# Moving the norm chains to the head of the next block, and regrouping the readout and one decay map in an RWKV-7 recurrence

## The reference, cut to what matters

```python
def rms_norm(x, g):
    y = xf * lax.rsqrt(jnp.mean(xf * xf, axis=-1, keepdims=True) + RMS_EPS)
...
    h_lat = h_lat + gt_m * o_lat
    f_lat = rms_norm(h_lat, norm_ffn[i]) * (1.0 + sc_f) + sh_f
    h_lat = h_lat + gt_f * swiglu(f_lat, ff_w1[i], ff_w3[i], ff_w2[i])
...
# RWKV-7: features, the chain of states, the readout
kk = kk / jnp.maximum(jnp.linalg.norm(kk, axis=-1, keepdims=True), NORM_EPS)
decay = _heads(jnp.exp(-jnp.exp(w_log)))
a = _heads(jax.nn.sigmoid((a0[:, None, None, :] + lora_a).astype(f32)))
...
S = (S * w_t[:, :, None, :] + sa[..., None] * (kk_t * a_t)[:, :, None, :]
     + v_t[..., None] * k_t[:, :, None, :])
...
yn = ((y - mean) * lax.rsqrt(var + LNX_EPS)).reshape(B, T, D) * lnx_g + lnx_b
bonus = jnp.sum(jnp.sum(r[None] * k_dir * r_k, axis=-1, keepdims=True) * v[None], axis=0)
g = jax.nn.sigmoid((h + xx * mu[5]) @ g1) @ g2
return ((yn + bonus.reshape(B, T, D)) * g).astype(h.dtype) @ wo
```

## Time and profile before

| what | us |
|---|---|
| median of 3 runs | 2176.03 |
| lowest and highest | 2170.07, 2177.54 |
| profiled execution, own time | 2173.98 |
| its span, first to last instruction | 2172.1 |
| PE busy in the span | 1988.3 (92%) |
| DVE, ACT, POOL busy | 1230.3, 836.8, 379.3 |
| recurrence, first to last step | 419 to 862 |

### The profile page before, as it was taken

How to read it: one execution, slowest core, us unless ns; L and a number is a source line. 1 busy time by engine, 2 the same in 40 slices (tenths; PEclk the granted TensorE clock), 3 DMA queues, 4 the chain that set the end, 5 groups by cost and what they waited for, 6 DMA issues and landing times. The chain is left out here.

```text
span 2172.1 us, 52627 instructions
## 1 busy us (share of the span) xinstructions
PE 1988.3 (92%) x22423; PEld 1739.4 (80%) x22423; DVE 1230.3 (57%) x1921; ACT 836.8 (39%) x1407; POOL 379.3 (17%) x394
## 2 busy tenths in 40 slices
PE   5799997789999988979999999997979898999998
PEld 3688886678888887979999999996635476888887
DVE  4765445667767763458756667564775434333333
ACT  2433334565565532344323324233335424422321
POOL 0000000766766652120000000022200010000000
PEclk8799998899999999989999999997989998999999
DMA  9577775101111001411212222212100023333332
GB/s 318 180 239 231 228 237 144 41 19 39 32 39 39 20 12 47 151 59 59 78 59 78 63 74 69 68 39 69 59 20 1 0 68 96 96 105 89 96 107 79
DMA packets 226985, 192.76 MB, mean 89 GB/s; under 512 B 13386, under 2 KB 211668, under 8 KB 226388
## 3 DMA queue, kind: packets, MB, share of 16 engines
q1 hardware_dynamic: 226452, 188.84, 28.1%
q0 software_dynamic: 320, 0.79, 0.2%
HBM read 171.38 MB, written 17.43 MB: 87 GB/s over the span
## 5 line engine op out<-in xcount | busy, mean ns | idle before, releaser
L539 DVE TENSOR_TENSOR ffn_lo<-ffn_raw,ffn_hi 128x1024 fp32r<-128x1024 f32 (+1 forms) x58 | 77.5, 1336 | 196.0 <-ACT ffn_hi L534 196.0
L563 PE MATMUL banks<-operand_hi,ffn_w_hi 128*128 128x384 f32 x464 | 155.7, 336 | 10.9 <-DVE operand_lo L505 10.9
L563 PE MATMUL banks<-operand_lo,ffn_w_hi 128*128 128x384 f32 x464 | 155.6, 335 | 0.0
L563 PE MATMUL banks<-operand_hi,ffn_w_lo 128*128 128x384 f32 x464 | 155.5, 335 | 0.0
L563 PE MATMUL banks<-mix_hi,proj_hi 128*128 128x386 f32 (+1 forms) x384 | 136.9, 356 | 15.4 <-DVE proj_lo L755 10.5
L563 PE MATMUL banks<-operand_hi,ffn_hi 128*128 128x512 f32 x352 | 138.4, 393 | 10.7 <-DVE operand_lo L505 8.4
L534 ACT CAST ffn_hi<-ffn_raw 128x1024 fp32r<-128x1024 f32 (+1 forms) x60 | 68.3, 1139 | 189.6 <-PE banks L563 182.6
L563 PE MATMUL banks<-operand_lo,ffn_hi 128*128 128x512 f32 x352 | 137.9, 392 | 0.0
L563 PE MATMUL banks<-operand_hi,ffn_lo 128*128 128x512 f32 x352 | 137.9, 392 | 0.0
L430 POOL TENSOR_TENSOR mix_and_norm<-mix_and_norm 128x768 f32<-128x768 f32 (+1 forms) x21 | 34.8, 1659 | 572.4 <-ACT mix_and_norm L424 572.4
L563 PE MATMUL banks<-mix_hi,proj_lo 128*128 128x386 f32 (+1 forms) x384 | 132.0, 344 | 0.0
(11 more groups left out here) (341 smaller groups left out, 5681.4 us busy)
## 6 DMA issues: line engine op xcount, KB each, us to landing
mod_raw<-in_mod_w SPq DMA_DIRECT2D x96, 512.0 KB, 5.2
ffn_raw<-in_ff_w SPq DMA_DIRECT2D x32, 1024.0 KB, 5.3
ffn_raw<-in_ff_w SPq DMA_DIRECT2D x46, 512.0 KB, 3.8
ffn_raw<-in_ff_w SPq DMA_DIRECT2D x16, 704.0 KB, 4.7
proj_raw<-in_rw_wr SPq DMA_DIRECT2D x16, 256.0 KB, 5.3
proj_raw<-in_rw_wk SPq DMA_DIRECT2D x16, 256.0 KB, 6.1
proj_raw<-in_rw_wv SPq DMA_DIRECT2D x16, 256.0 KB, 6.1
rwkv_out_raw<-in_rw_wo SPq DMA_DIRECT2D x8, 512.0 KB, 4.2
```

The costliest lines, as they stand in the source:

```text
L539: signal(eng, eng.tensor_tensor(self.lo[s][:, 0:k_tiles, :], self.raw[s][:, 0:k_tiles, :], self.hi[s][:, 0:k_tiles, :].bitcast(F32), ALU.s ...
L563: mm = pe.matmul(out, a, b, start=(first and n == 0), stop=(last and n == 2), skip_group_check=onto)
```

## The change

**Norm chains.** `last_square`, `sums`, `root`, `invert` and `spread` leave the end of `rwkv_out`, `feed_forward_seven` and `dense` and stand at the head of `feed_forward_seven`, `qkv` and `feed_forward`, ahead of everything else that PE, ACT and DVE do there. The table's preload stays where it was. `sums` uses bank 0 now. POOL in `feed_forward_seven` waits for the sums before it clears `pool_sum` for the next norm.

**Recurrence.** `y_sum`, `y_root`, `y_invert`, `y_spread` and `y_scale` (until now in the last steps of the period before), `y_bonus`, `gate` and `gated` come later, beside `kk_root`, `map2`, `map1`, `sigmoid1` and `scan0` of the same period. `map0` and `sigmoid0` come later too, right behind `map2` and `sigmoid2`. `t_copy(at(5), 3)` goes ahead of `kk_root`. A third bonus buffer is there, and `bonus` waits for `y_bonus` of t-3.

```diff
-    def sums(self, pe, bank):
+    def sums(self, pe):
+        bank = self.c.bank[0]
...
-    def root(self, act, bank):
+    def root(self, act):
...
-        bonus = [*(sb(f"bonus{s}", [P, TOK]) for s in range(2)), full[0][:, 0:TOK]]
-        bonus_of = lambda t: bonus[2 if t == CT - 1 else t % 2]
+        bonus = [*(sb(f"bonus{s}", [P, TOK]) for s in range(3)), full[0][:, 0:TOK]]
+        bonus_of = lambda t: bonus[3 if t == CT - 1 else t % 3]
...
+                t_copy(at(5), 3)
+                feature_of(pair, "y_sum")
                 feature_of(pair + 3, "kk_root")
...
-                            after(dve, use, t - 2, "y_bonus")
+                            after(dve, use, t - 3, "y_bonus")
...
                 by_two(pe, 0, CT // 2, pair)
-                norm.sums(pe, c.bank[6])
-                norm.spread(pe)
...
                 norm.table(act)
-                act.wait_ge(added, ns * CT)
-                norm.last_square(act)
-                norm.root(act, c.bank[6])
...
+                norm.sums(pe)
+                norm.spread(pe)
                 halves(pe, tile, outputs)
...
+                norm.invert(dve)
                 norm.scale(dve, 0)
...
+                pool.wait_ge(norm.summed, norm.number + 1)
                 following.clear(pool)
```

More of the change, by code:

```diff
@@ L451, in sums @@
         mm.then_inc(self.summed, 1)
-    def root(self, act, bank):
+    def root(self, act):
         n = len(self.blocks)
         act.wait_ge(self.summed, self.number + 1)
-        act.activation(self.rows[:, 0:n], bank[:, 0:n], ACT.Sqrt, scale=1.0 / D, bias=self.c.eps[:, 0:1])\
+        act.activation(self.rows[:, 0:n], self.c.bank[0][:, 0:n], ACT.Sqrt, scale=1.0 / D, bias=self.c.eps[:, 0:1])\
             .then_inc(self.rooted, 1)
@@ L1262, in period @@
                 mask(at(6), 1)
+                t_copy(at(5), 3)
+                feature_of(pair, "y_sum")
                 feature_of(pair + 3, "kk_root")
                 cut(at(5), 4)
-                t_copy(at(5), 3)
+                feature_of(pair, "y_root")
+                feature_of(pair, "y_invert")
                 feature_of(pair + 3, "map2")
                 feature_of(pair + 3, "sigmoid2")
+                feature_of(pair + 3, "map0")
+                feature_of(pair + 3, "sigmoid0")
                 decay(at(4), 1)
@@ L1272, in period @@
                 rhs_copy(at(4), 1)
+                feature_of(pair, "y_spread")
                 y(at(5), 3)
+                feature_of(pair, "y_scale")
                 keys(at(6))
@@ L1282, in period @@
                 diag(at(8))
+                feature_of(pair, "gate")
                 products(at(4), 1)
@@ L1287, in period @@
                 update(at(4), 1)
+                feature_of(pair, "y_bonus")
                 feature_of(pair + 3, "kk_invert")
@@ L1292, in period @@
                 rhs(at(4), 2)
+                feature_of(pair, "gated")
                 values(at(6))
@@ L2569, in outputs @@
                             finish(half, HT - 1, 0, s)
+                norm.last_square(act)
+                norm.root(act)
                 halves(act, tile, outputs)
@@ L3031, in add @@
                             self.frees(("down", part, m, q), added, 3 * self.of("added", part, m))
[L3033 to L3037, removed]
+                norm.sums(pe)
+                norm.spread(pe)
+                schedule(Pe())
             @block.scalar
@@ L3088, in following @@
                         following.square(act, m, m % 2)
-                act_part = Act()
-                schedule(act_part)
+                norm.last_square(act)
+                norm.root(act)
+                schedule(Act())
                 following.table(act)
-                act.wait_ge(added, 3 * act_part.of("added", PARTS - 1, CT - 1))
-                following.last_square(act)
-                following.root(act, sum_bank(act_part))
             @block.gpsimd
```

16 lines of the change are left out of this document (1 added, 15 removed).

## The result

The changed kernel takes 2200.69 us (median of 4 runs, 2199.59 to 2201.79) against 2174.89 before: a ratio of 1.0118, 95% interval 1.0105 to 1.0132. It is 25.8 us slower, and outside the range that was given (2160 to 2194). Its profiled span is 2199.9 us, 27.8 more than before.

What follows compares the result with a forecast made beforehand. PE was taken as nearly the bound in the recurrence, a norm-and-load chain at the seams. From 2173.98: -14.0 seams, +17 recurrence passes, +1 ends, +3 SP's queue, -1 covered waits, giving 2180 us; range 2160 to 2194.

Steps and rivals of the forecast that it cites:

- The seams: Three block heads: weight load issued beside the norm chain, first products earlier by 4.2, 6.3 and 3.5 us, together -14.0.
- The place to which the readout goes: Two later recurrence steps: 5.6 us of PE work plus four new waits totalling 2.3, +7.9 us a pass.
- SP's queue: Map-weight loads queued behind the store that waits for `gated`: ACT waits 1.6 us, +0.8 in four passes, +3.
- The place that it leaves: Three recurrence steps losing 5.56 us of PE work: -4.5 us a pass, between -2.8 and -5.6.
- Passes 6 and 7: End of the recurrence: readout 5 and the `kk_root` with its load behind `t_copy`, put at +1 in all.
- The sum: Whole kernel: 2173.98 - 14.0 + 17 + 1 + 3, less 1 for short PE waits covered by new ones: 2180 us.
- (B): Rival: in the recurrence moved work costs what it frees, only the seams' gain remains, 2160 us; chance 0.22.
- (C): Rival: ACT's table loads were on the path, 15.4 us more come off than in (B), 2145 us; chance 0.04.
- the 46 and 34 of the signs: Sign to look for in the changed kernel's timeline: 34 table loads in place of 46.
- (D): Rival: `gated` ends 2 us later than worked out, paid by `values` and `map_round`, 2192 us; chance 0.26.
- (E): Rival: DVE and POOL pace the block heads, so the seams give nothing, 2194 us, or 2174 with (B); chance 0.06.
- over 62: Sign: a recurrence pass longer than 62 us would mean (D); no longer than 58 us would mean (B).

Runs made afterwards that it cites:

- n_only: Only the norm chains' part of the change, the recurrence as in the kernel before: ratio 0.9946 to the kernel before, 2162.97 us.
- after_sp: The changed kernel with the next pair's map weights loaded ahead of the store that waits for `gated`: ratio 1.0098 to the kernel before.
- n_readout: The changed kernel with `map0` and `sigmoid0` left at their old place, the readout moved: ratio 1.0122 to the kernel before.
- n_map0: `n_only` with only `map0` and `sigmoid0` moved behind `sigmoid2`, the readout left in place: ratio 0.9961 to the kernel before.
- n_trim: `n_only` with the readout's three groups of PE matmuls cut to one each at their old place, output wrong: ratio 0.9884 to the kernel before.
- after_gate_later: The changed kernel with `gate` and `gated` put behind `values` and the copy of `values` a little earlier: ratio 1.0108 to the kernel before.
- n_tail: `n_only` with only `y_bonus`, `gate` and `gated` moved to their new places, with the third bonus buffer: ratio 0.9996 to the kernel before.
- after_fill: The changed kernel with two useless large products ahead of the keys of each third group: ratio 1.0100 to the kernel before.
- after_fill_small: The changed kernel with 96 useless 64x64 products ahead of the keys of each third group: ratio 1.0297 to the kernel before.
- after_trim: The changed kernel with the readout's three matmul groups cut to one each at their new place, output wrong: ratio 1.0017 to the kernel before.

## Why the prediction was wrong

- **The seams**: right. Forecast 4.2 + 6.3 + 3.5, found 3.4 + 6.0 + 3.5, and `n_only` confirms the sum. The first was too high since the sums ran at half clock (0.50 from 985 to 991; 2.70 us for L450 where 1.50 had stood), which the low part, hardly beside POOL now (1.42 for two), gave back in part.
- **The place to which the readout goes**: right in sum, +7.9 forecast and +7.8 to +8.1 found in steps 5 to 7 of passes 1 to 5, with all four waits at the places named (PE idle 12.1 us there in five passes, 0.4 before): 0.2, 0.6, 0.3, 1.2 forecast, 0.3, 0.5, 0.4, 1.2 in the list.
- **SP's queue**: right in kind, 4 passes with a wait on the map weights, but the wait was 2.7 us in all for the 1.6 x 4 of the working, and it was paid nearly in full (`after_sp` gives 2.6 back), not by half. That the 3 in the sum fits is luck: two errors cancel.
- **The place that it leaves**: wrong, and the larger miss. The term was -4.5 a pass, -22.5 for five; found are -2.9, -2.1, -2.9, 0.0, -3.0, together -10.9. The failing step is the sum 2.8 + 1.0 + 0.64, all three terms of it. The first pass had shown 2.8 for the readout's 4.59 us; `n_readout`, which moves just these, gives 1.8 back. "`map 0` brings 1.0 more" holds for map 0 alone (`n_map0`: 0.9 for its 0.97), but on top of the readout it brings 0.5 (the changed kernel against `n_readout`). And the wait of 0.64 for the copy of `rhs` was one of the first pass: in passes 1 to 5 PE had no such wait there. What the working left out is what PE meets next when its own work goes: PE waits for nothing shown for 9.6 us in these stretches of passes 1 to 5 where it had 3.1 before, by the packets a wait for its instructions, and both fillers hid 10 us and more there; with the work only cut down, not moved (`n_trim`), it meets ACT's `sigmoid0` instead, 4.2 us. The half clock in passes 2 to 4 can't be much of it: `after_gate_later` has none there, and steps 2 to 4 are only 0.2 to 0.6 us shorter in these passes.
- **Passes 6 and 7**: wrong. Readout 5 was put at +1 and readout 6 at nothing; found are +3.0 and +4.1 (and +1.0 in pass 0). These passes have fewer features, so I had taken the moved work as even. But steps 5 to 7 grow by 3.8 and 4.7 there, and steps 2 to 4 give 2.3 and 0.6 back: there too less comes back than is added.
- **The sum**: -14.0 + 21 - 1 had been 6; -12.9 + 38.9 is 26. Of the 19 us by which the recurrence was short (38.9 for 20), 12 are the first of the two wrong terms and 7 the second; the rest is within 1 us by differences of opposite sign.
- **The rivals**: (B) failed: the steps that the readout left gave 10.9 us back in passes 1 to 5, those to which it went took 39.8. (C) failed: `n_map0` takes 12 table loads away too, without the readout's move, and is no faster than `n_only`. (The lines view counts 54 loads before and 42 after in the whole kernel; the 46 and 34 of the signs were miscounted.) The rule of 2.66 us a switch in the Trainium skill ("ScalarE: Activation LUTs", "What ACT_TABLE_LOAD costs") would have had 32 us of ACT go. The trace doesn't agree: ACT is busy for 820.7 us in place of 836.8, so 16.1 went, 12 x 1.283 being 15.4. Before, a load stood at 544.00 for 1.28 us; the copy ahead of it ended at 543.99 and the sigmoid behind it began at 545.30, with no room for a drain. (D) named the right instruction, but its wait had the size of the forecast, not more; the time passed its 2192 for another reason. (E) failed.
- A pass "over 62" was to tell (D): passes 1 to 5 last 62.0 to 67.6 us, and the sign was thus ambiguous; the list of waits was what told the causes apart.

What stays open: 11 of the head's 27 us lie in passes 0, 6 and 7 (`n_readout` against `n_tail`), and no run says what makes them. Nor was a kernel run whose instructions come sooner, so the waits for them rest on the traces' timing and on the two fillers.

## What to carry to other kernels

Work moved between two places of a list can have a different price at each: cut it down at the old place first and see what the time gives back, before counting that as the gain, and don't add gains that were seen one by one. An engine's work beside a table switch or a run of small products may cost nothing just because it covers them, so to save switches pays only where the switch is waited for. A few long products among many short ones also give the instruction queue time; when idle time without a releaser grows, look where that queue's packets start. A chain that doesn't need the next block's loads can go behind the barrier with them; here that gave 3.4 of 6.3, 6.0 of 7.3 and 3.5 of 4.7 us from square to load.

## What the runs showed of the hardware that was not expected

- In stretches of dense 64x64 products PE stood idle up to 2.6 us at a time for nothing that the profile shows as a releaser, and each such idle time of 0.6 us and more in the recurrence (15 to 24 a run, in all 14 traces) ended 2.2 to 3.0 us after the start of a 16 KB packet of the instruction queue. Of 12.5 us of 128-wide products laid into such stretches 0.4 showed, of 51.0 us of 64-wide ones 40.5.
- The granted clock fell to half (1.2 of 2.4 GHz) for 3.4 us in four passes of the changed kernel, each time behind an idle time of 1.74 to 2.56 us. Such an idle time isn't needed for it: the one fall in the recurrence of `n_only` has none over 0.3 us in the 8 us ahead, and 1.72 us of idle time ahead of 788.6 us in the changed kernel brought none. `after_fill`, `after_fill_small`, `n_tail` and `after_trim` have no fall.
- The sums over the last square, 12 products of one column, took 1.50 us at the first seam before and 2.70 after, the same work, at a granted clock of 1.00 and 0.50; after, PE had been idle for 1.90 us behind the barrier just ahead of the norm's other sums. At the second seam they took 2.59 already before.
